# Four splitting steps of the retention heads moved from ScalarE and VectorE to GpSimd

## What is computed

```python
def retention_chunk(S, q, k, v):
    ...
    scores = jnp.einsum('bihd,bjhd->bhij', q, k) * decay[None]
    o_intra = jnp.einsum('bhij,bjhe->bihe', scores, v)
    o_cross = jnp.einsum('bihd,bhde->bihe', q, S) * q_dec[None, :, :, None]
    S_new = (jnp.exp(C * lg)[None, :, None, None] * S
             + jnp.einsum('bjhd,bjhe->bhde', k * k_dec[None, :, :, None], v))
    return S_new, o_intra + o_cross

def retention_layer(x, pos, S0, chunk, norm_w, w_in, gn_w, w_out):
    h = rmsnorm(x, norm_w) @ w_in
    q, k, v, g = jnp.split(h, [qk_w, 2 * qk_w, 2 * qk_w + RET_VW], axis=-1)
    ...  # rotary on q and k, four heads of 256 (k) by 512 (v)
    o = rmsnorm(o, gn_w).reshape(B, T, RET_VW)
    y = (o * jax.nn.silu(g)) @ w_out
    return x + y, S_fin
```

## Time and profile before

| what | us |
|---|---|
| median of 3 executions (524.07 to 524.96) | 524.5 |
| the profiled execution's own time | 524.96 |
| its span (first to last instruction) | 523.2 |
| PE busy | 515.1 |
| DVE busy | 342.4 |
| ACT busy | 257.7 |
| POOL busy | 72.2 |

### The profile page before, as it was taken

One profiled execution on the slowest core, in us unless ns is written; L12 is line 12 of the kernel. 1 busy time (PEld: TensorE's weight loads), 2 busy tenths in 40 slices (PEclk: granted clock), 3 DMA queues, 4 the chain that ended last, 5 costly groups with the idle time before them and its releaser, 6 DMA issues.

```text
span 523.2 us, 9484 instructions
## 1 busy us (share of the span) xinstructions
PE 515.1 (98%) x3595; PEld 445.2 (85%) x3595; DVE 342.4 (65%) x628; ACT 257.7 (49%) x511; POOL 72.2 (14%) x81
## 2 busy tenths in 40 slices
PE   7999999999999999999999999999999999999997
PEld 6889977899779977897899999988887778999886
DVE  2775448892878738892698967645756764776531
ACT  5826442572338532562743455744444655555520
POOL 0291004420091004420000130100000000000000
PEclk9999999999999999999999999999999999999999
DMA  7983979999999999989747966516797557682211
GB/s 223 361 303 133 267 243 344 382 297 229 323 352 322 225 262 321 378 264 212 235 147 274 337 195 230 172 52 241 232 337 242 206 187 242 237 299 105 81 50 51
DMA packets 78865, 125.52 MB, mean 240 GB/s; under 512 B 3859, under 2 KB 41828, under 8 KB 78692
## 3 DMA queue, kind: packets, MB, share of 16 engines
q1 hardware_dynamic: 78738, 124.89, 74.1%
q10 hardware_dynamic: 82, 0.02, 0.0%
HBM read 98.93 MB, written 27.57 MB: 242 GB/s over the span
## 4 chain that ended last, share of the span: by engine, by line
PE 86%; ACT 5%; DVE 5%; DMA 2%; issue 1%; ACTq 0%; SPq 0%; DVEq 0%
PE bank L823 37%; PE bank L820 19%; PE bank L809 7%; PE bank L988 3%; PE bank L934 3%; DVE w_lo L1433 2%; PE bank L1002 2%; ACT w_hi L1118 2%; PE bank L1055 1%; PE bank L952 1%; PE bank L906 1%; DMA w_raw<-in_ret_w_in 1%; PE bank L893 1%; PE bank L835 1%; PE bank L1094 1%
## 5 line engine op out<-in xcount | busy, mean ns | idle before, releaser
L1433 DVE TENSOR_TENSOR w_lo<-w_raw,w_hi 128x512 fp32r<-128x512 f32 x206 | 145.1, 742 | 72.1 <-ACT w_hi L1118 71.8
L1118 ACT ACTIVATE w_hi<-w_raw 128x512 fp32r<-128x512 f32 x208 | 118.6, 620 | 49.4 <-PE bank L823 22.2
L823 PE MATMUL bank<-xn_hi,w_hi 128*128 128x320 f32 x320 | 100.6, 318 | 0.9 <-DVE w_lo L1433 0.5
L823 PE MATMUL bank<-xn_hi,w_lo 128*128 128x320 f32 x320 | 97.6, 309 | 0.0
L823 PE MATMUL bank<-xn_lo,w_hi 128*128 128x320 f32 x320 | 97.5, 309 | 0.0
L820 PE MATMUL bank<-w_hi,xn_hi 128*128 128x512 f32 x160 | 65.6, 410 | 0.0
L823 PEld LDWEIGHTS bank<-xn_hi,w_hi 128*128 128x128 f32 x320 | 59.7, 188 | 4.6 <-issue 2.8
L820 PE MATMUL bank<-w_lo,xn_hi 128*128 128x512 f32 x160 | 62.7, 392 | 0.0
L820 PE MATMUL bank<-w_hi,xn_lo 128*128 128x512 f32 x160 | 62.5, 391 | 0.0
L823 PE MATMUL bank<-ym_hi,w_hi 128*128 128x320 f32 x192 | 61.8, 322 | 0.0
L823 PEld LDWEIGHTS bank<-xn_lo,w_hi 128*128 128x128 f32 x320 | 59.8, 188 | 0.5
(11 more groups left out here) (228 smaller groups left out, 743.9 us busy)
## 6 DMA issues: line engine op xcount, KB each, us to landing
w_raw<-in_ret_w_in SPq DMA_DIRECT2D x23, 1024.0 KB, 10.8
st<-in_state_ret SPq DMA_DIRECT2D x32, 512.0 KB, 8.2
out_ret_state_sample<-st SPq DMA_DIRECT2D x32, 512.0 KB, 4.7
w_raw<-in_ret_w_out SPq DMA_DIRECT2D x8, 1024.0 KB, 9.2
w_raw<-in_moba_w_in SPq DMA_DIRECT2D x8, 1024.0 KB, 6.7
cache<-in_cache_k SPq DMA_DIRECT2D x16, 512.0 KB, 5.2
w_raw<-in_w_kv SPq DMA_DIRECT2D x8, 1024.0 KB, 6.1
cache<-in_cache_v SPq DMA_DIRECT2D x16, 512.0 KB, 4.5
```

What stands on the lines that cost most here:

```text
L823: mm = pe.matmul(bank[out][:, 0:T], w[:, wk, P * tile:P * tile + P], x[:, k, :], **flags)
L1118: act.activation(w_hi[:, c % 2, part], w_raw[:, c % RAW, part], ACT.Copy).then_inc(w_hi_done, 1)
L1433: dve.tensor_tensor(w_lo[:, c % 2, part], w_raw[:, c % RAW, part], w_hi[:, c % 2, part].bitcast(F32), ALU.subtract).then_inc(w_lo_done, 1)
```

## The change

Four operations go to POOL. `vp_hi` and `kd_hi` were ACT's in step `SC`, and are now copies on POOL in that step. `kd_lo` was DVE's in step `OP`, and is now POOL's in step `SC`, behind `kd_hi`. `vs_lo` was one fused multiply-and-subtract on DVE, and is now two POOL instructions, a multiplication and a subtraction with a wait between, at the third tile of `rv`. Nothing is computed less, and the list of steps is the same.

```diff
@@ ACT @@
-                elif kind == "SC":
-                    h = step[1]
-                    await_read(act, *tile_use("rv", 3 * h + 1))
-                    if h:
-                        await_full(act, 5, "SS", h - 1)
-                    act.activation(vp_hi, vp[:, :, :], ACT.Copy).then_inc(vp_hi_done, 1)
-                    await_read(act, 3, "KT", h)
-                    await_full(act, 5, *step)
-                    act.activation(kd_hi, kd[:, :, :], ACT.Copy).then_inc(kd_hi_done, 1)
@@ DVE @@
-            def own_values_lo(h):
-
-                dve.wait_ge(vs_hi_done, h + 1)
-                dve.scalar_tensor_tensor(vs_lo[:, :], vs[:, :], rms[0:TS, 2:3], vs_hi[:, :].bitcast(F32), ALU.mult, ALU.subtract)\
-                    .then_inc(vs_lo_done, 1)
...
-                        if h == 0:
-                            await_read(dve, b, *step[:3])
-                            own_values_lo(h)
...
-                    dve.wait_ge(kd_hi_done, h + 1)
-                    dve.tensor_tensor(kd_lo[:, :, :], kd[:, :, :], kd_hi.bitcast(F32), ALU.subtract).then_inc(kd_lo_done, 1)
...
-                    if step[1] < RH - 1:
-                        await_read(dve, *tile_use("rv", 3 * step[1] + 5))
-                        own_values_lo(step[1] + 1)
@@ POOL @@
+                elif kind == "TILE" and chunks[step[1]][0] == "rv" and step[2] == 2:
+                    h = chunks[step[1]][1]
+                    pool.wait_ge(vs_hi_done, h + 1)
+                    done(pool.tensor_scalar(vs_lo[:, :].bitcast(F32), vs[:, :], rms[0:TS, 2:3], None, ALU.mult))
+                    done.wait()
+                    pool.tensor_tensor(vs_lo[:, :], vs_lo[:, :].bitcast(F32), vs_hi[:, :].bitcast(F32), ALU.subtract)\
+                        .then_inc(vs_lo_done, 1)
...
+                elif kind == "SC":
+                    h = step[1]
+                    for t in range(2):
+                        await_read(pool, *tile_use("rv", 3 * h + t))
+                    if h:
+                        await_full(pool, 5, "SS", h - 1)
+                    else:
+                        pool.wait_ge(roots_done, 2)
+                    pool.tensor_copy(vp_hi, vp[:, :, :]).then_inc(vp_hi_done, 1)
+                    await_read(pool, 3, "KT", h)
+                    await_full(pool, 5, *step)
+                    pool.tensor_copy(kd_hi, kd[:, :, :]).then_inc(kd_hi_done, 1)
+                    pool.wait_ge(kd_hi_done, h + 1)
+                    pool.tensor_tensor(kd_lo[:, :, :], kd[:, :, :], kd_hi.bitcast(F32), ALU.subtract).then_inc(kd_lo_done, 1)
```

## The result

The changed kernel takes 528.4 us (median of 6, 527.66 to 529.29) where the kernel before takes 524.51 (median of 6): a ratio of 1.0074, 95% interval 1.0061 to 1.0087. It is 3.9 us slower. The forecast was no change, 523.7 to 526.2; it was wrong, and the time is that of the second rival, 528.4.

What follows compares the result with a forecast made beforehand. PE's matmul stream was taken to bound the four heads, so relief of ACT and DVE and the work moved to POOL each counted 0: 524.96 - 0 + 0, predicted against the median as 524.5 us, range 523.7 to 526.2.

Steps and rivals of the forecast that it cites:

- Rival 2: Heads 1 to 3: DVE, fully blocked by POOL, 3.2 us late, stalls PE ahead of `OP`; 528.4 us, chance 0.09.
- PE bounds the heads, and relief of ACT and DVE is worth nothing: Four retention heads, 24 to 245 us: PE busy 221.0 of 221.0 us, so relieving ACT and DVE gains 0 us.
- What POOL gets, 6.0 us a head: Five new POOL instructions a head: 6.0 us, 24 us in all; undisturbed ends 4.5 and 7.6, disturbed up to 17.4.
- In time for `SF` and `vp_lo`: Head 1: `vp_hi` ends 5 us before `vp_lo` needs it, `kd_lo` 5.4 us before `SF`; no wait.
- Rival 3: POOL's `kd_lo` late for PE's `SF` if new work takes over 12.7 us: up to 541.3 us, chance 0.04.
- The SP queue, 3.0 us in hand: Weight load behind the stores of `vs_lo` and `ks_lo`: `vs_lo` may be done 3 us later before PE notices.
- The cost on DVE: Head 1 before bank 5's reading: three meetings with POOL at 0.49 us, DVE 0.8 us late against 1.9 in hand.

Runs made afterwards that it cites:

- only pauses added: The changed kernel with four semaphore waits more on GpSimd, each on its own last instruction, no work added: 525.17 us, ratio 1.0007.
- part kernels: Four kernels moving only part of the change (`vs_lo` back, `kd_lo` back, two copies only, `vs_lo` only), against the kernel before: 524.68, 524.92, 525.0, 525.54 us.
- copies without a pause: The changed kernel with an added GpSimd copy of `vp` into `fin` ahead of `vp_hi`, no wait between: 531.57 us, ratio 1.0139.

## Why the prediction was wrong, point by point

- *PE bounds the heads, and relief of ACT and DVE is worth nothing:* right. The kernels with a part of the relief, and the one with all of it (only pauses added), are not faster. ACT's `ym_hi` did start earlier, at 109.48 instead of 113.08, for nothing.
- *What POOL gets, 6.0 us a head:* nearly right as a sum, 6.9 us in head 1 (1.56 + 2.10 + 1.03 + 0.61 + 1.61), two of them held by DVE; POOL was busy for 95.2 us in all, 96 were forecast. The copies lay near the lower end, 1.03 and 0.61 us. The multiplication by a scalar took 1.56 us, above the upper bound of 1.29 that I had taken from the two-input rate.
- *In time for `SF` and `vp_lo`:* right. `kd_lo` ended at 115.07, and PE never waited for POOL. Rival 3 did not happen.
- *The SP queue, 3.0 us in hand:* enough for the change. It was counted for PE's wait on the weight chunk alone; DVE's update of `st` behind the chunk had only some 0.9 us, and two of the part kernels lost 0.5 us there once.
- *The cost on DVE:* this is the step that failed. It took 0.49 us for each meeting, the mean over four pieces beside the rotation, and said DVE would be 0.8 us late against 1.9 in hand. Measured were 1.8, 1.25 and 1.1 us for three pieces, and 2.96 us late. The mean hid that a piece is held to the end of the POOL instruction that it meets, and sometimes through the next one as well. I also counted the wrong ones: the 128x1280 product ran at 1.49 us, and it was POOL's `vs_lo` that paid (2.10 instead of 1.34 us in head 0), while the pair at 109.26, which I left out as having met `ks_lo` and `qz` already, grew from 1.83 to 3.22 us under `vs_lo`.
- *Rival 2:* its mechanism, its threshold of 1.9 us and its three heads were right, and its price of 1.3 us a head is near the 1.19 measured. That its 528.4 is met to the tenth is in part luck. Its 3.2 us of lateness was 2.3 (`vs_lo`) + 1.6 (`vp_hi`) - 0.7; measured were 1.8 (`vs_lo` and `ks_lo`), 1.25 (`vp_hi` and `kd_hi`) and 1.1 (`kd_lo`), less what the pieces had paid before and less `vs_lo`. Of the loss of a head, 0.7 us falls on the fourth `w_lo` piece, which it hadn't named. The fault was its chance of 0.09 beside a row that already showed `ks_lo` at 0.74 and 1.70 us.
- *Slips without weight:* from 121.38 to 125.10 there are 3.7 us, not 3.6; `vs_hi` ends at 105.92 and 46.20, not 105.99 and 46.27, as rival 3 has it; and PE had two waits of 0.5 us for DVE, not one.
- The Trainium skill's rule on the shared interface (SBUF — State Buffer, Who interferes with whom), that each blocks the other for a whole instruction and that a GpSimd instruction which only writes does not take part, was weighed and then set aside for the mean. The trace agrees with both halves for POOL's copies and two-input instructions (pieces that end 0.54 us after one of them has ended) and for memsets (a piece of 0.68 us beside two of them), but not for the multiplication by a scalar, which reads SBUF and let a piece run inside it in 0.86 us.

## What to carry to other kernels

An instruction moved to an idle engine is not free if that engine shares an interface with a busy one: before moving, list the two-input instructions of VectorE that will stand beside it, give each a whole hold (the rest of the GpSimd instruction that it meets, and of the next ones if they follow without a pause), and set the sum against the time in hand of the next consumer. If the move is wanted all the same, choose its place by who is beside it, and leave pauses in GpSimd's sequence. A time in hand makes parts look free one by one, so the sum must be tried as a whole.

## What the runs showed of the hardware that was not expected

- GpSimd instructions that follow each other without a pause can hold a waiting two-input instruction of VectorE like one long instruction: a piece of 0.68 us took 2.49 us through two of them (the changed kernel) and 4.02 us through five (copies without a pause). They need not: at 166 places without a pause a piece got in, at 72 it was passed over.
- At a pause of GpSimd, down to 0.06 us, no waiting piece was passed over. Four more semaphore waits of GpSimd on its own instructions, and nothing else, took the changed kernel from 528.4 (ratio 1.0074) to 525.2 us (ratio 1.0007).
- GpSimd's multiplication by a per-partition scalar took 1.56 us for 64x512, more than a two-input subtraction of that size (1.34 us); its copies took 0.61 us for 512 and 1.03 us for 1024 elements. A two-input piece of VectorE that fell inside this multiplication took 0.86 us, so it was not held to its end; the held pieces beside other GpSimd instructions were.
